# A two-block fp32 network on one core: halved peer_v weights ahead of their tiles, a chunk-major gather, slot gates on expert outputs, and an early memory norm

## The chip, the cores and the metric

One NeuronCore of a Trainium2 chip. The metric is the device time of one execution in microseconds (us); lower is better. Engines are called PE (TensorE), ACT (ScalarE), DVE (VectorE), POOL (GpSimd) and SP (SyncE, which here only issues DMAs).

## What is computed

256 tokens of width 1024 pass through two transformer blocks, all in fp32. The parts that matter here, cut from the reference:

```python
# block 1: stick-breaking attention and spatial gating, then 4 groups x 8 experts (1024 x 512)
combine = (g_onehot[:, :, None] * (g_weight[:, None] * e_w)[:, None, :]).astype(x.dtype)  # top 1 group, top 2 experts
for g in range(N_GROUPS):
    h = silu(einsum('nd,edf->nef', xt, w_gate[g])) * einsum('nd,edf->nef', xt, w_up[g])
    out = out + einsum('nef,efd->nd', h * combine[:, g, :, None], w_down[g])
# block 2
merged = sigmoid(gate_a) * (o_a @ w_branch_a) + sigmoid(gate_b) * (o_b @ w_branch_b)
h = h + merged @ w_out
h = h + memory_cross_attention(rms_norm(h, norm_cross), rms_norm(mem, norm_mem), w_cross_q, w_cross_kv, w_cross_o)
# peer_ffn: 16384 experts; each token takes 16 of them in each of 8 heads
act = gelu(einsum('cd,chkd->chk', xc, u_tab[ec]))
out = einsum('chk,chkd->cd', gc * act, v_tab[ec])
```

## The kernel before, in words

**Products.** A full fp32 product on PE is four passes. Most large products here are three fp32r matmuls instead (`three`, L194): each operand is split into a rounded HIGH part, which ACT copies (`high_quarters` L173, `high` L1713, `weight_high` L1993), and a LOW rest, which DVE subtracts (`low_quarters` L180, `low` L1730, `weight_low` L2032). The experts' own weights stay plain fp32. All matmuls are issued at L189 (`mm`), all transposes at L192 (`tr`).

**Order.** Every engine has its program written out by hand; `Steps` numbers the steps of an engine on one semaphore, and others wait for a step with `.at(name)`. SP loads all large weights in one order through slots of 2 MB (`load_piece` L165).

**Experts (143 to 663 us).** Expert `ex` owns 64 slots. For each, `experts_pe` (L585) runs gate and up (32 fp32 matmuls, 8 chunks x 2 x 2; the trace has two records for each fp32 matmul), `add(ex-1)` (L610: the 64x128 placing matrix times the output rows of the expert before, into four banks that gather all experts), two transposes of h, the turning of the placing matrix `PC` (one-hot x gate weight `CB`, made by `places_dve` L739), a quarter of the gather of the next four experts (`gather_pe` L576: 8 matmuls whose weights are the halved normed tokens, `XGH` and `XH` in the rows, read at every 8th column), and the product with w_down (y). ACT does silu and the copy `hp` (h turned and placing turned); DVE does h = silu x up, the gathered rows, and `YS`, the copy of y. Three weight pieces of 2 MB per expert come through seven slots.

**Seam and mixers of block 2 (663 to 905 us).** After the last add DVE adds four 128x512 residual pieces (L804), the norm follows, and PE starts on block 2's input projection in pieces b0 to b9 of w_in. High and low of b0 and b1 stand at the end of the experts' code.

**Branches and cross attention (905 to 1058 us).** `branches`: for each half of the tokens four products with w_branch, each followed by DVE's `sa`, `sb`, `sx`. Then `cross_pe` (L1428): turn of the merged rows, w_out in two halves (`residual`, o20 and o21), with the turn of the normed memory `turnm` between, K of the memory (kv0), turn of the normed tokens, V (kv1), Q (cq). mem is loaded at L1481 ff. by ACT's queue after the last merged row.

**Dense PEER (1121 to 1950 us).** 128 "up" tiles of peer_u, then 128 "down" tiles of peer_v. SP loads tile i, ACT makes TH (three buffers), DVE makes TL (five buffers). An up tile's gelu goes to DRAM (`g_hold`) and comes back in the down phase into `GL` (four buffers); POOL multiplies it by the router's weights `C`; ACT makes WH and DVE WL (two buffers each), the weights of the down tile's 12 matmuls of 128x512. The loops of ACT and DVE:

```python
for i in range(255):                       # ACT
    if i + 2 < 256:
        high(act, i + 2)                   # TH of tile i+2
    if i >= 127:
        weight_high(i - 127)               # WH of down tile i-127; waits for down tile i-129
for i in range(lows_made.count, 257):      # DVE
    if i < 256:
        low(dve)                           # TL of tile i
    if i >= 129:
        weight_low(i - 129)                # WL of down tile i-129
```

`high(act, i + 2)` waits until the tile three before it has been used, so both steps of ACT in one turn of the loop wait for the same down tile of PE. SP issues the read of g_hold for down tile j when it comes to tile j+129, behind a wait for the WL of four tiles before.

## Time and profile before

| what | us |
|---|---|
| three runs | 1958.85, 1956.11, 1966.63 |
| their median | 1958.85 |
| the profiled execution's own time | 1964.08 |
| its span | 1962.3 |
| PE busy | 1814.5 (92%) |
| DVE, ACT, POOL busy | 927.3, 680.3, 310.2 |
| mean granted TensorE clock, of full speed | 0.954 |

The page cuts the span into 40 slices of 49 us, a digit for the busy tenths:

```profile
PE   6977999999999598999878999999999999999997
...
PEclk9987999999999897579989999999999999999999
DMA  7128999999999435013433177755556766666664
```

PE is busy nearly throughout. DMA is at nine tenths only in slices 5 to 13, the experts; it has room elsewhere. The clock falls below nine tenths between slice 14 and slice 19, in the seam and the mixers of block 2. A matmul's row shows its latency in the pipeline, so the spacing of the starts of a run of matmuls, not a row's mean, tells what each costs.

### The profile page before, as it was taken

Reading aid. Unit: us, or ns where it says so; the run is one execution under the profiler, and the core shown is the slowest. Engines: PE = TensorE matmul, PEld = TensorE weight load, DVE = VectorE, ACT = ScalarE, POOL = GpSimd, SP = SyncE. Lnnn points to the kernel's source line nnn. Section 1 sums busy time; section 2 is a strip of 40 time slices with the busy share of each in tenths; the row PEclk is TensorE's granted clock in tenths of the full one; section 3 lists DMA queues with packets and bytes.
Section 4 is the critical chain, followed back from the end, with each engine's and each line's share of the span. In section 5 each row is a group of like instructions: output and inputs, shape, how many; then the busy total and the mean of one; then the engine's idle time right before and its main releaser. Section 6 shows DMA issues by size and latency. Waiting matters only on the chain.

```text
span 1962.3 us, 27788 instructions
## 1 busy us (share of the span) xinstructions
PE 1814.5 (92%) x11296; PEld 1402.2 (71%) x11296; DVE 927.3 (47%) x1753; ACT 680.3 (35%) x1143; POOL 310.2 (16%) x289
## 2 busy tenths in 40 slices
PE   6977999999999598999878999999999999999997
PEld 6765555555555396566676999999999766666665
DVE  4533111111111433654524899666665566666665
ACT  5720000000000243452334444555554444444443
...
PEclk9987999999999897579989999999999999999999
DMA  7128999999999435013433177755556766666664
GB/s 312 67 98 367 393 403 413 398 403 408 406 402 418 179 129 215 1 44 129 193 129 118 54 229 228 217 176 175 176 176 188 232 208 207 203 206 203 207 203 130
DMA packets 99651, 443.60 MB, mean 226 GB/s; under 512 B 10432, under 2 KB 43712, under 8 KB 79424
## 3 DMA queue, kind: packets, MB, share of 16 engines
...
## 4 chain that ended last, share of the span: by engine, by line
PE 82%; DVE 9%; ACT 6%; DMA 1%; issue 1%; ACTq 0%; DVEq 0%
PE PS L189 79%; DVE TL L1734 4%; PE PS L192 3%; ACT TH L1717 3%; DVE WL L2034 1%; DMA AR<-in_mem 1%; DVE LO L185 1%; ACT HI L178 0%; DMA AR<-in_w_out 0%; DVE XL L248 0%; ACT XSs L255 0%; DMA Hs<-in_x 0%; DVE Wk L261 0%; DVE AR L261 0%; DVE Wk L1352 0%
## 5 line engine op out<-in xcount | busy, mean ns | idle before, releaser
L1734 DVE TENSOR_TENSOR TL<-Wk,TH 128x1024 fp32r<-128x1024 f32 x256 | 357.9, 1398 | 280.1 <-ACT TH L1717 280.0
L1717 ACT ACTIVATE TH<-Wk 128x1024 fp32r<-128x1024 f32 x256 | 270.1, 1055 | 230.6 <-PE PS L189 230.6
L189 PE MATMUL PS<-XH,TH 128*128 128x256 f32 x1024 | 295.1, 288 | 0.8 <-DVE TL L1734 0.8
L189 PE MATMUL PS<-XL,TH 128*128 128x256 f32 x1024 | 289.6, 283 | 0.0
L189 PE MATMUL PS<-XH,TL 128*128 128x256 f32 x1024 | 289.5, 283 | 0.0
L189 PE MATMUL PS<-TH,WH 128*128 128x512 f32 x512 | 211.7, 414 | 25.7 <-DVE WL L2034 22.7
L189 PE MATMUL PS<-AR,Wk 128*64 128x512 f32 (+5 forms) x848 | 216.2, 587 | 6.0 <-ACT Wk L685 2.1
L189 PE MATMUL PS<-AR 128*64 128x256 f32 (+2 forms) x1912 | 208.2, 389 | 6.1 <-ACT AR L1192 2.5
L189 PE MATMUL PS<-TH,WL 128*128 128x512 f32 x512 | 202.7, 396 | 0.0
L189 PE MATMUL PS<-TL,WH 128*128 128x512 f32 x512 | 202.2, 395 | 0.0
L189 PEld LDWEIGHTS PS<-XH,TH 128*128 128x128 f32 x1024 | 196.2, 192 | 1.0 <-DVE TL L1734 1.0
L189 PEld LDWEIGHTS PS<-XL,TH 128*128 128x128 f32 x1024 | 196.4, 192 | 0.0
L189 PEld LDWEIGHTS PS<-XH,TL 128*128 128x128 f32 x1024 | 196.1, 191 | 0.0
L189 PEld LDWEIGHTS PS<-AR 128*64 128x64 f32 (+1 forms) x1912 | 134.5, 141 | 85.1 <-issue 18.4
L2072 POOL TENSOR_TENSOR CO<-CO,AR 128x256 f32<-128x256 f32 x128 | 142.6, 1114 | 304.4 <-DMA CO<-g_hold 304.4
L189 PEld LDWEIGHTS PS<-TH,WH 128*128 128x128 f32 x512 | 96.0, 187 | 91.2 <-DVE TL L1734 44.3
L185 DVE TENSOR_TENSOR LO<-AR,HI 128x1024 fp32r<-128x1024 f32 x96 | 111.6, 1226 | 102.1 <-ACT HI L178 102.1
L189 PEld LDWEIGHTS PS<-AR,Wk 128*64 128x64 f32 (+2 forms) x848 | 79.4, 168 | 108.9 <-issue 95.3
L683 ACT ACTIVATE AR<-PS 128x256 f32<-128x256 f32 x32 | 12.3, 383 | 392.5 <-PE PS L189 392.5
L2018 POOL TENSOR_SCALAR RW<-CO,Wk 128x128 f32<-128x128 f32 x128 | 104.1, 823 | 183.2 <-PE PS L189 129.1
L189 PEld LDWEIGHTS PS<-TH,WL 128*128 128x128 f32 x512 | 96.2, 188 | 23.1
L1987 ACT ACTIVATE Wk<-PS 128x256 f32<-128x256 f32 x128 | 49.1, 384 | 179.9 <-PE PS L189 179.8
...
## 6 DMA issues: line engine op xcount, KB each, us to landing
Wk<-in_peer_u SPq DMA_DIRECT2D x128, 512.0 KB, 3.8
Wk<-in_peer_v SPq DMA_DIRECT2D x128, 512.0 KB, 3.8
...
g_hold<-Wk SPq DMA_DIRECT2D x128, 128.0 KB, 3.7
CO<-g_hold SPq DMA_DIRECT2D x128, 128.0 KB, 3.7
```

The costliest lines, as they stand in the source:

```text
L185: eng.tensor_tensor(lo[:, cs], w[:, cs], hi[:, cs].bitcast(F32), ALU.subtract).then_inc(*steps.up(f"{name}.{k}"))
L189: return pe.matmul(o, l, r, start=start, stop=stop, skip_group_check=True)
L192: return pe.transpose(o, i, ident[0:n, 0:n])
L683: act.activation(SG[:, b, :], G[:, 0:256], ACT.Silu).then_inc(*m_act.up(f"silu{ex}"))
L1717: act.activation(TH[:, i % 3], RAW[:, i % 5], ACT.Copy).then_inc(t_high, 1)
L1734: dve.tensor_tensor(TL[:, i % 5], RAW[:, i % 5], TH[:, i % 3].bitcast(F32), ALU.subtract).then_inc(*lows_made.up())
L1987: act.activation(GE[i % 3], P(4 + i % 4)[:, 0:256], ACT.Gelu).then_inc(gelu_done, 1)
L2018: return eng.tensor_scalar(o, io, I1T[:, tok:tok + 1], GTT[:, tok:tok + 1], ALU.is_equal, ALU.mult)
L2034: dve.tensor_tensor(WL[:, j % 2, :], GL[j % 4], WH[:, j % 2, :].bitcast(F32), ALU.subtract).then_inc(w_low, 1)
L2072: pool.tensor_tensor(GL[j % 4], GL[j % 4], C[:, :, j], ALU.mult).then_inc(gated, 1)
```

## The change

- **Dense down.** ACT makes WH ahead of TH, DVE makes WL ahead of TL. GL has seven buffers in place of four, and SP reads g_hold three tiles earlier.
- **Experts.** The normed tokens are written in chunk-major order (one DVE operation per half reads H at every 8th column), so the gather and the first transposes read contiguous columns. PC is gone; the one-hot matrix PG itself is turned, and DVE copies it rounded into PT2 (`hr`). The gate weight of each slot is summed by four matmuls of one column (`gate_of_slots`), which DVE copies to SLOT_GATE (`gs`) before it makes h; y is multiplied by it and halved: ACT writes YH, DVE YL. `add` is then two fp32r matmuls (YH, YL) for each of its four pieces in place of one fp32 matmul.
- **Seam.** The halving of b0 moves into the last expert, b1's high behind it and b1's low behind the split of the turned tokens (`turn_dve` x).
- **Memory.** mem is loaded by SP right after the first block's norm, normed while PE does the gate pieces b6 to b9, and turned between the two halves of the branches. kv0 takes o20's place in the order of loads; its products come first in cross_pe, V comes before the turn of the normed tokens.

Cut to what matters (list names, waits of the same kind and the layout of buffers are left out):

```diff
-                    t = mm(pe, o[:, k, :], halves[n % 2][:, tt, 2 * s + k::8], PG[:, b, tt, :], n == 0, n == 3)
+                    t = mm(pe, o[:, k, :], halves[n % 2][:, tt, (2 * s + k) * 128:(2 * s + k) * 128 + 128], PG[:, b, tt, :], n == 0, n == 3)
...
-                        t = tr(pe, bank[:, k, tt * 128:(tt + 1) * 128], XS[:, tt, 2 * pair + k::8])
+                        t = tr(pe, bank[:, k, tt * 128:(tt + 1) * 128], XS[:, tt, (2 * pair + k) * 128:(2 * pair + k) * 128 + 128])
...
                         r = slice(64 * j, 64 * j + 64)
-                        t = mm(pe, P(2 * tt + j), HP[r, b, 256 + tt * 128:384 + tt * 128], YS[r, b, :], ex == 0, ex == 31)
+                        to = PT2[r, b, tt * 128:tt * 128 + 128]
+                        mm(pe, P(2 * tt + j), to, YH[r, b, :], ex == 0, False)
+                        t = mm(pe, P(2 * tt + j), to, YL[r, b, :], False, ex == 31)
                 t.then_inc(*m_pe.up(f"add{ex}"))
+            def gate_of_slots(ex):
+
+                g, k4 = ex // 4, ex % 4
+                if ex:
+                    pe.wait_ge(*m_dve.at(f"hr{ex - 1}"))
+                for tt in range(2):
+                    pg = PG[:, g % 2, tt, k4 * 64:k4 * 64 + 64].bitcast(F32)
+                    for j in range(2):
+                        t = mm(pe, P(5 - ex % 2)[64 * j:64 * j + 64, 0:1], pg, CB[:, tt, ex:ex + 1], tt == 0, tt == 1)
+                t.then_inc(*m_pe.up(f"gsum{ex}"))
...
-                if ex >= 2:
-                    pe.wait_ge(*m_act.at(f"hp{ex - 2}"))
...
+                gate_of_slots(ex)
                 pe.wait_ge(*m_dve.at(f"h{ex}"))
...
                 for tt in range(2):
-                    pc = PC[:, g % 2, tt, k4 * 64:k4 * 64 + 64]
+                    pg = PG[:, g % 2, tt, k4 * 64:k4 * 64 + 64].bitcast(F32)
                     for j in range(2):
-                        t = mm(pe, G[64 * j:64 * j + 64, 256 + tt * 128:384 + tt * 128], pc, ident, True, True)
+                        t = mm(pe, G[64 * j:64 * j + 64, 256 + tt * 128:384 + tt * 128], pg, ident, True, True)
                 t.then_inc(*m_pe.up(f"turned{ex}"))
...
+                if ex == 31:
+                    act.wait_ge(*m_pe.at("gate31"))
+                    high_quarters(act, "b0", b_act, range(3))
                 act.wait_ge(*m_pe.at(f"up{ex}"))
                 act.activation(SG[:, b, :], G[:, 0:256], ACT.Silu).then_inc(*m_act.up(f"silu{ex}"))
                 act.wait_ge(*m_pe.at(f"turned{ex}"))
-                act.activation(HP[:, b, :], G, ACT.Copy).then_inc(*m_act.up(f"hp{ex}"))
-            act.wait_ge(*m_pe.at("gate31"))
-            high_quarters(act, "b0", b_act)
-            act.wait_ge(*m_pe.at("up31"))
+                act.activation(HP[:, b, :], G[:, 0:256], ACT.Copy).then_inc(*m_act.up(f"hp{ex}"))
+                if ex == 31:
+                    high_quarters(act, "b0", b_act, range(3, 4))
+                act.wait_ge(*m_pe.at(f"y{ex}"))
+                act.activation(YH[:, b, :], P(6), ACT.Copy, scale=SLOT_GATE[:, b:b + 1]).then_inc(*m_act.up(f"ysh{ex}"))
...
-                dve.wait_ge(*m_dve.at(f"pg{g}.{tt}"))
-                dve.tensor_tensor(pc, pg.bitcast(F32), bc(CB[:, tt, 4 * g:4 * g + 4].unsqueeze(2), [128, 4, 64]), ALU.mult).then_inc(
-                    *m_dve.up(f"pc{g}.{tt}"))
...
-                t = scaled(dve, XS[:, tt, :], H[:, tt, :], ST[:, tt:tt + 1])
+                by_chunk = H[:, tt, :].rearrange("p (n c) -> p c n", c=8)
+                t = scaled(dve, XS[:, tt, :].rearrange("p (c n) -> p c n", c=8), by_chunk, ST[:, tt:tt + 1])
...
+                if ex == 31:
+                    low_quarters(dve, "b0", b_act, b_dve, range(2))
+                dve.wait_ge(*m_pe.at(f"gsum{ex}"))
+                dve.tensor_copy(SLOT_GATE[:, b:b + 1], P(5 - b)[:, 0:1]).then_inc(*m_dve.up(f"gs{ex}"))
                 dve.wait_ge(*m_act.at(f"silu{ex}"))
                 dve.tensor_tensor(HM[:, b, :], SG[:, b, :], P(4 + b)[:, 256:512], ALU.mult).then_inc(*m_dve.up(f"h{ex}"))
+                dve.wait_ge(*m_act.at(f"hp{ex}"))
+                dve.tensor_copy(PT2[:, b, :], P(4 + b)[:, 256:512]).then_inc(*m_dve.up(f"hr{ex}"))
                 if g < 7:
                     gathered_dve(dve, g + 1, k4)
-                dve.wait_ge(*m_pe.at(f"y{ex}"))
-                dve.tensor_copy(YS[:, b, :], P(6)).then_inc(*m_dve.up(f"ys{ex}"))
-            low_quarters(dve, "b0", b_act, b_dve)
-            low_quarters(dve, "b1", b_act, b_dve)
+                if ex == 31:
+                    low_quarters(dve, "b0", b_act, b_dve, range(2, 4))
+                dve.wait_ge(*m_act.at(f"ysh{ex}"))
+                dve.scalar_tensor_tensor(YL[:, b, :], P(6), SLOT_GATE[:, b:b + 1], YH[:, b, :].bitcast(F32), ALU.mult,
+                                         ALU.subtract).then_inc(*m_dve.up(f"ys{ex}"))
...
-            for name, step in (("b2", m_pe.at("up30")), ("b3", m_pe.at("y30")), ("b4", b_pe.at("q3")), ("b5", b_pe.at("k3")),
+            for name, step in (("b2", m_pe.at("up30")), ("b3", m_pe.at("y30"))):
+                sp.wait_ge(*step)
+                load_piece(sp, name)
+            sp.wait_ge(*m_dve.at("normed"))
+            sp.dma_start(MM, mem.rearrange("(t p) d -> p t d", p=128)).then_inc(ld_mem, 16)
+            for name, step in (("b4", b_pe.at("q3")), ("b5", b_pe.at("k3")),
                                ("ck0", b_pe.at("va1")), ("ck1", b_pe.at("qb3")), ("b6", b_pe.at("kv3")), ("b7", b_pe.at("vb1")),
                                ("b8", b_pe.at("cmp")), ("b9", b_pe.at("cmp")), ("wa", b_pe.at("g01")), ("wb", b_pe.at("g11")),
-                               ("o20", b_pe.at("g21")), ("o21", b_pe.at("g31"))):
+                               ("kv0", b_pe.at("g21")), ("o20", b_pe.at("g31"))):
...
+                if tt == 0:
+                    pe.wait_ge(*b_dve.at("mem"))
+                    pe.wait_ge(*b_act.at("g31"))
+                    turn_pe(pe, MM).then_inc(*b_pe.up("turnm"))
...
+            act.wait_ge(ld_mem, 16)
+            square_sum(act, MM[:, 0, :], junk[:, 0, :], ST[:, 24:25]).then_inc(*b_act.up("sqm"))
...
+                if j == 0:
+                    act.wait_ge(*b_dve.at("meanm"))
+                    act.activation(ST[:, 24:26], ST[:, 24:26], ACT.Sqrt).then_inc(*b_act.up("rootm"))
...
+            high_quarters(act, "kv0", b_act)
+            act.wait_ge(*b_pe.at("turnm"))
+            turn_act(act, MX2, sm["g_mem"], b_act, "m")
             high_quarters(act, "o20", b_act)
-            high_quarters(act, "o21", b_act)
...
             turn_dve(dve, X2, sm["g_nmix"], b_act, b_dve, "x")
+            low_quarters(dve, "b1", b_act, b_dve)
             lam = sm["lam"]
             for i in range(2):
                 t = dve.tensor_tensor_reduce(S4[:, i, 0:64], lam[:, 128 * i:128 * i + 64], lam[:, 128 * i + 64:128 * i + 128], 1.0, 0.0,
...
-            for name in ("b7", "b8", "b9", "o20", "o21"):
-                low_quarters(dve, name, b_act, b_dve)
+            dve.wait_ge(ld_mem, 16)
+            square_sum_dve(dve, MM[:, 1, :], junk[:, 1, :], ST[:, 25:26]).then_inc(*b_dve.up("ssm"))
+            dve.wait_ge(*b_act.at("sqm"))
...
+            for tt in range(2):
+                t = scaled(dve, MM[:, tt, :], MM[:, tt, :], ST[:, 24 + tt:25 + tt])
+            t.then_inc(*b_dve.up("mem"))
...
+            branches(0)
+            low_quarters(dve, "kv0", b_act, b_dve)
+            turn_dve(dve, MX2, sm["g_mem"], b_act, b_dve, "m")
+            branches(1)
+            low_quarters(dve, "o20", b_act, b_dve)
...
-            for name, step in (("kv0", b_pe.at("b11")), ("kv1", b_pe.at("b11")), ("cq", c_pe.at("r01")), ("co", c_pe.at("r11")),
-                               ("pq0", c_pe.at("k3")), ("pq1", c_pe.at("v1"))):
+            for name, step in (("o21", b_pe.at("b11")), ("kv1", b_pe.at("b11")), ("cq", c_pe.at("k3")), ("co", c_pe.at("r01")),
+                               ("pq0", c_pe.at("r11")), ("pq1", c_pe.at("v1"))):
                 sp.wait_ge(*step)
...
         def cross_pe(pe):
+            for m in range(4):
+                if m >= 2:
+                    pe.wait_ge(*c_act.at(f"k{m - 2}"))
+                turned(pe, "kv0", MX2, P(m % 2)[:, 0:256], m, *((b_dve, b_dve, "m") if m == 0 else ())).then_inc(*c_pe.up(f"k{m}"))
             pe.wait_ge(*b_dve.at("sx11"))
+            pe.wait_ge(*c_act.at("k3"))
             turn_pe(pe, XS).then_inc(*c_pe.up("turnx"))
-
-            def residual(j):
+            for j, lows in ((0, b_dve), (1, c_dve)):
                 for tt in range(2):
-                    tokens(pe, f"o2{j}", X2, P(4 + 2 * j + tt), tt, *((b_dve,) if tt == 0 else ()),
+                    tokens(pe, f"o2{j}", X2, P(4 + 2 * j + tt), tt, *((lows,) if tt == 0 else ()),
                            *((c_dve, "x") if j + tt == 0 else ())).then_inc(*c_pe.up(f"r{j}{tt}"))
-
-            residual(0)
-            pe.wait_ge(*c_dve.at("mem"))
-            turn_pe(pe, MM).then_inc(*c_pe.up("turnm"))
-            residual(1)
+            for tt in range(2):
+                tokens(pe, "kv1", MX2, P(tt), tt, *((c_dve,) if tt == 0 else ())).then_inc(*c_pe.up(f"v{tt}"))
+            pe.wait_ge(*c_dve.at("zs"))
+            pe.wait_ge(*c_act.at("v1"))
+            turn_pe(pe, XS).then_inc(*c_pe.up("turnz"))
             for m in range(4):
-                pe.wait_ge(*(c_act.at(f"k{m - 2}") if m >= 2 else c_dve.at(f"r0{m}")))
-                turned(pe, "kv0", MX2, P(4 + m % 2)[:, 0:256], m, *((c_dve, c_dve, "m") if m == 0 else ())).then_inc(*c_pe.up(f"k{m}"))
-            pe.wait_ge(*c_dve.at("zs"))
-            turn_pe(pe, XS).then_inc(*c_pe.up("turnz"))
-            for tt in range(2):
-                pe.wait_ge(*c_dve.at(f"r1{tt}"))
-                tokens(pe, "kv1", MX2, P(6 + tt), tt, *((c_dve,) if tt == 0 else ())).then_inc(*c_pe.up(f"v{tt}"))
-            for m in range(4):
-                pe.wait_ge(*c_act.at(f"q{m - 2}" if m >= 2 else f"k{m + 2}"))
+                pe.wait_ge(*(c_act.at(f"q{m - 2}") if m >= 2 else c_dve.at("r11")))
...
-                j = i - 129
+                j = i - 126
                 if 0 <= j < 128:
                     if j == 0:
                         sp.wait_ge(pairs, 64)
                     sp.wait_ge(g_out[j % 3], 16 * (j // 3 + 1))
-                    if j >= 4:
-                        sp.wait_ge(w_low, j - 3)
-                    sp.dma_start(GL[j % 4], g_hold[j]).then_inc(g_in[j % 4], 16)
+                    if j >= 7:
+                        sp.wait_ge(w_low, j - 6)
+                    sp.dma_start(GL[j % 7], g_hold[j]).then_inc(g_in[j % 7], 16)
...
             for i in range(255):
+                if i >= 127:
+                    weight_high(i - 127)
                 if i + 2 < 256:
                     high(act, i + 2)
                 if i == LOWS_BEFORE_SUB:
                     gates_exp_act(act)
-                if i >= 127:
-                    weight_high(i - 127)
...
             for i in range(lows_made.count, 257):
+                if i >= 129:
+                    weight_low(i - 129)
                 if i < 256:
                     low(dve)
                 if 0 <= i - TAKE - 1 < 64:
                     marks(i - TAKE - 1)
-                if i >= 129:
-                    weight_low(i - 129)
```

On ACT, where the up tiles change to the down tiles; TH is the high part of a table tile, WH that of a down tile's weights, and the writes to Wk or RW from PS are gelus. Before:

```order
L1717 ACTIVATE TH<-Wk 128x1024
L1987 ACTIVATE Wk<-PS 128x256
L1717 ACTIVATE TH<-Wk 128x1024
L1997 ACTIVATE WH<-CO 128x256
L1987 ACTIVATE Wk<-PS 128x256
L1717 ACTIVATE TH<-Wk 128x1024
L1997 ACTIVATE WH<-CO 128x256
```

and now:

```order
L2024 ACTIVATE RW<-PS 128x256
L2034 ACTIVATE WH<-CO 128x256
L1754 ACTIVATE TH<-Wk 128x1024
L2024 ACTIVATE RW<-PS 128x256
L2034 ACTIVATE WH<-CO 128x256
L1754 ACTIVATE TH<-Wk 128x1024
L2034 ACTIVATE WH<-CO 128x256
```

The WH copy stands ahead of the TH copy of its turn; behind the last gelu the two alternate in both kernels.

On PE, one expert between gate/up and the gather. Before:

```order
L189 MATMUL PS<-AR,Wk 64x512 x8
L189 MATMUL PS<-AR 64x256 x32
L189 MATMUL PS<-AR,Wk 128x512 x4
L192 MATMUL PS<-CO,AR 128x128 x2
L189 MATMUL PS<-CO,Wk 64x128 x4
L189 MATMUL PS<-PG,XGH 128x256
```

and now:

```order
L189 MATMUL PS<-AR,Wk 64x512 x8
L189 MATMUL PS<-AR 64x256 x32
L189 MATMUL PS<-YH,PT_59 128x512
L189 MATMUL PS<-YL,PT_59 128x512
...
L189 MATMUL PS<-Wk,PG 64x1 x4
L192 MATMUL PS<-CO,AR 128x128 x2
L189 MATMUL PS<-CO,PG 64x128 x4
L189 MATMUL PS<-PG,XGH 128x256
```

YH and YL alternate four times. The four matmuls of one column are new and stand between the add and the transposes of h.

On DVE, the last expert and the seam (AR written from PS is h, L797 the copy of y, Hs the residual, LO the low parts of w_in, XL that of the turned tokens). Now:

```order
L185 TENSOR_TENSOR LO_51<-AR,HI_49 128x1024 x2
L811 COPY Wk<-PS 128x1
L813 TENSOR_TENSOR AR<-AR,PS 128x256
L815 CAST PT_59<-PS 128x256
L185 TENSOR_TENSOR LO_51<-AR,HI_49 128x1024 x2
L821 SCALAR_TENSOR_TENSOR YL<-PS,Wk,YH 128x512
L827 TENSOR_TENSOR Hs<-PS,Hs 128x512 x4
...
L248 SCALAR_TENSOR_TENSOR XL<-PS,SM,XH 128x256 x8
L185 TENSOR_TENSOR LO_52<-AR,HI_50 128x1024 x4
```

Before, all eight lows of L185 stood between the copy of y and the residual adds; now four stand ahead of it and four behind the split of the turned tokens.

## Rows read from the trace of the kernel before

**Rows 1.** Table by stretch: us; busy and count of each engine; clock, DMA share, GB/s

```profile
521.61:537.00 15.39, 15.39 (x107) 9.01 (x106) 1.99 (x4) 0.98 (x2) 0.00 (x0) 1.00 1.00 412
1540.00:1950.00 410.00, 385.13 (x1536) 278.59 (x1536) 257.19 (x254) 171.97 (x253) 140.86 (x126) 1.00 0.65 201
```

**Rows 2.** Groups by line, down phase 1540 to 1950: busy us, mean ns, idle before

```profile
L189 PE MATMUL PS<-TH,WH 128*128 128x512 f32 x512 | 211.7, 414 | 25.7 <-DVE WL L2034 22.7 <-issue 0.9
L1734 DVE TENSOR_TENSOR TL<-Wk,TH 128x1024 fp32r<-128x1024 f32 x126 | 191.4, 1519 | 146.9 <-ACT TH L1717 146.9
L2072 POOL TENSOR_TENSOR CO<-CO,AR 128x256 f32<-128x256 f32 x126 | 140.9, 1118 | 261.5 <-DMA CO<-g_hold 261.5
```

**Rows 3.** Timeline of one down tile: start, duration (us), engine, what, idle before

```profile
1700.44 1.06 ACT L1717 ACTIVATE TH<-Wk 128x1024 fp32r<-128x1024 f32 x1 [2.20 <-PE PS L189]
1700.67 0.40 PE L189 MATMUL PS<-TL,WH 128*128 128x512 f32 x1
1700.80 0.88 POOL L2072 TENSOR_TENSOR CO<-CO,AR 128x256 f32<-128x256 f32 x1 [0.87 <-DMA CO<-g_hold]
1701.41 0.40 ACT L1997 ACTIVATE WH<-CO 128x256 fp32r<-128x256 f32 x1
1701.54 1.23 DVE L1734 TENSOR_TENSOR TL<-Wk,TH 128x1024 fp32r<-128x1024 f32 x1 [1.33 <-ACT TH L1717]
1702.68 0.41 DVE L2034 TENSOR_TENSOR WL<-CO,WH 128x256 fp32r<-128x256 f32 x1
1703.00 0.40 PE L189 MATMUL PS<-TH,WL 128*128 128x512 f32 x1
```

**Rows 4.** Timeline of one expert, PE and the h of DVE

```profile
356.51 7.08 PE L189 MATMUL PS<-AR 128*64 128x256 f32 x64
363.52 1.99 PE L189 MATMUL PS<-AR,Wk 64*128 64x512 f32 x8
364.05 0.42 DVE L793 TENSOR_TENSOR AR<-AR,PS 128x256 f32<-128x256 f32 x1 [5.05 <-ACT AR L683]
365.44 0.50 PE L192 MATMUL PS<-CO,AR 128*128 128x128 f32 x2
366.46 0.51 PE L189 MATMUL PS<-PG,XGH 128*128 128x256 f32 x1
368.60 3.65 PE L189 MATMUL PS<-AR,Wk 128*64 128x512 f32 x16
372.08 3.62 PE L189 MATMUL PS<-Wk,AR 128*64 128x256 f32 x32
```

**Rows 5.** Groups of weight loads on PE, whole kernel: busy us, mean ns, idle before

```profile
L189 PEld LDWEIGHTS PS<-XH,TL 128*128 128x128 f32 x1024 | 196.1, 191 | 0.0
L189 PEld LDWEIGHTS PS<-PG,XH 128*128 128x128 f32 x128 | 43.3, 339 | 0.0
```

**Rows 6.** Timeline of SP and DVE, last experts and seam

```profile
626.90 0.38 SPq L171 DMA_DIRECT2D Wk<-in_w_down  x1
...
662.59 0.69 DVE L797 COPY AR<-PS 128x512 f32<-128x512 f32 x1 [6.46 <-PE PS L189]
663.20 9.16 DVE L185 TENSOR_TENSOR LO<-AR,HI 128x1024 fp32r<-128x1024 f32 x8
672.28 2.47 DVE L804 TENSOR_TENSOR Hs<-PS,Hs 128x512 f32<-128x512 f32 x4
...
688.22 3.23 DVE L248 SCALAR_TENSOR_TENSOR XL<-PS,SM,XH 128x256 fp32r<-128x256 f32 x8 [5.03 <-ACT XH L241]
```

**Rows 7.** Timeline of PE from the branches to the cross attention

```profile
920.67 14.00 PE L189 MATMUL PS<-AR,Wk 128*128 128x512 f32 x32 [1.38 <-DVE AR L1385]
936.18 2.06 PE L192 MATMUL PS<-CO,XSs 128*128 128x128 f32 x16 [1.50 <-DVE XSs L1387]
955.38 3.68 PE L192 MATMUL PS<-CO,AR 128*128 128x128 f32 x16 [4.38 <-DVE AR L261]
```

**Rows 8.** Chain of waits, the one piece between those rows: start, us, what

```profile
936.15 14.83 DMA AR<-in_mem
```

**Rows 9.** Page, DMA issues of this kind: count, KB each, us to landing

```profile
CO<-g_hold SPq DMA_DIRECT2D x128, 128.0 KB, 3.7
```

146 lines of the change are left out of this document (69 added, 77 removed).

## The prediction

> **What bounds the kernel now.** I read the table by stretch first, then the groups by line, the timelines, and the chain of waits last. The span is PE's nearly everywhere, so a part gains only where it takes matmuls off PE or closes a gap on it. Two long stages stand out. In the experts a stretch of 15.39 us has PE busy throughout and the DMAs at their full share, 412 GB/s [rows 1]: PE and DMA both bind. In the down phase PE is busy 385.13 of 410.00 us with DMA at 0.65 [rows 1], and one group carries the idle time, 25.7 us in front of the matmuls by WH, nearly all released by DVE's WL [rows 2]. The busy time hides more than that. From the second matmul of a tile (1700.67) to its twelfth (1703.00) there are ten steps of 0.233 us [rows 3], so a tile needs 12 x 0.233 = 2.80 us, and it gets 410.00/128 = 3.20. The other 0.2 us per tile lie in the last matmul's row, which lasts 0.40 while the next could start after 0.233.
>
> **Dense down.** What makes a tile late: when PE has done tile j-2, ACT may write TH of tile j+1 and only then WH of tile j (1700.44 and 1701.41); on DVE the low of the table (1.23 us, 1.519 on average) stands before WL (1702.68) [rows 2, 3]. In series that is 1.06 + 1.23 + 0.41 and handovers of about 0.15 = 2.85 us at best, 3.14 with the mean of TL, and PE has only tile j-1, 2.80 us, to do meanwhile. Handovers on PE make it 3.20. Afterwards the chain from tile j-2 is WH 0.40 + WL 0.41 + handovers, about 1 us, or 1.9 if POOL's 0.88 [rows 3] stands in its way. Either is under 2.80. TH and TL fall back by 0.4 us, but TH has three buffers and is needed a whole tile later: done(j-2) + 0.40 + 1.06 + 1.52 = 3.0 us, against 5.6 until tile j+1 begins. Nothing on ACT (1.46 us a tile) or DVE (1.93 to 2.11) is near 2.80. So PE becomes the bound; I take 2.82 a tile: 128 x (3.20 - 2.82) = **-48.6 us**. Bounds: -25.7, only the idle time of the group [rows 2], and -51. The longer ring of GL is costed at nothing: POOL waits for its reads (261.5 us [rows 2]), but a read lands in 3.7 us [rows 9] and is issued about two tiles and PE's backlog ahead; it covers the WH copy that is now earlier.
>
> **Experts, per expert.** A period is 372.08 - 356.51 = 15.57 us: gate and up 7.01, add 1.92, transposes and turning 1.02, gather 2.14, y 3.48 [rows 4].
> - add: four fp32 matmuls of four passes take 1.92, so 16 passes at 0.12: the two 64-row halves run beside each other. Now 8 passes of 0.233 in 4 slots plus a tail of 0.18 are 1.11: -0.81. Bound: no overlap, 8 x 0.233, nothing gained.
> - gate_of_slots: four fp32 matmuls of one column. The nearest row is the group of two transposes and four turning matmuls, 1.02 [rows 4]; four sixths are 0.68. With one column in place of 128 I take 0.30; bounds 0.1 and 0.68.
> - h: it used to run under the add (364.05, before 365.44 [rows 4]). It now waits for the sums and for `gs`, so PE's transposes wait: the drain of the last matmul 0.17 to 0.25, gs at most 0.42 (h itself has 256 columns and takes 0.42 [rows 4]) and taken as 0.2, h 0.42: +0.9 of idle PE; bounds 0.7 and 1.2.
> - gather: 8 matmuls of 256 columns. Half of 0.233 would do, but each takes 0.24: the weight load takes 339 ns where contiguous ones take 191 [rows 5]. If the load shrinks, 8 x 0.12 = 0.96 goes; bound: nothing goes.
> - YH, YL, PT2 and HP lie on ACT and DVE under 7 us of gate and up: nothing. SP's queue keeps its order.
>
> Sum -0.81 + 0.30 + 0.90 - 0.96 = -0.57 for each of the 28 experts that gather, -16.0. The last four have no gather: +0.39, less 0.22 since y there waits for the copy hp, now half as wide (a 128x1024 copy takes 1.06 and a 128x256 one 0.40 [rows 3], 0.22 for 256 columns): +0.7. At the start PC goes (-0.4) and the normed tokens are written from a strided read (+0.7). **-15.0 us.** Bounds -27 and +12.
>
> Here a page speaks against part of it. The 16 transposes at 936.18 read at stride 8 too and take 2.06 us, 0.13 each [rows 7]; a load of 339 ns has no room there. So stride alone does not set the price, and whether the gather's loads shrink is open. The Trainium skill (SBUF — State Buffer, section "Door 1", its note on cachelines) says that each access that leaves a 16-byte line pays, so that fp32 can be strided by up to 4 elements for free. By it the gather gains, as I took; the transposes would gain too, which that row denies, and DVE's strided read would cost more than I took.
>
> Does DMA allow 15.0? Three pieces of 2 MiB (6.29 MB) at 412 GB/s need 15.27 us. The shortfall of 0.27 adds up to 7.6 us over 28 experts. But the last w_down is issued at 626.90 and is needed at 662.59 - 3.5 = 659.1 [rows 6], while the three pieces under way then need at most 15.3: the lead is 17 us. It covers that.
>
> **Seam.** Eight lows (9.16 us) stand between the copy of y and the residual adds at 672.28 [rows 6]. Four are now done in the last expert and four later, so the adds start when y31, YH, YL and the last add are done: 662.54 + 0.6 + 0.7 + 1.1 + handovers = 665.6: -6.7. b1's four lows (4 x 1.145 = 4.6) now follow DVE's split at 688.22 [rows 6] and hold up the small lambda work, for which ACT's copies of q wait: +2.0, bounds 0 and 4.6. **-4.7 us.**
>
> **Memory and cross.** Gone from PE's path: the wait for `sb` 1.38 and for the merged rows 1.50, the wait for the normed memory 4.38, and part of turnm's 3.68 us, which is so long since the clock had fallen in the 14.83 us in which the path waited for mem [rows 7, 8]; at full clock 16 transposes take 2.06 [rows 7]. That is 1.38 + 1.50 + 4.38 + 1.6 = 8.9, and some 1.8 for the half-speed matmuls behind that wait and for the wait of k. New are waits for the evacuation of k and v (0.45 + 0.7) and for the second norm, with V alone (6 us) to hide it: 1.9. The norm of mem on ACT and DVE hides under PE's gates; if b7's highs come late by a square and two table loads, that costs 1 to 2 us, which I put into the range. **-8 us**, bounds -2 and -12.
>
> **Sum**: 48.6 + 15.0 + 4.7 + 8 = 76.3, so 1964.1 - 76.3 = 1887.8 against the profiled execution's own time. The median of the runs shown stands 5.2 below that time, which would give 1882.6. I forecast **1885**.
>
> **Rivals.**
> - *The experts gain nothing.* Either the gather keeps its 0.24 a matmul (28 x 0.96 = 27 us back), for which the transposes speak, or the halves of the add do not overlap in their new order YH, YL of one half, then of the other (31 x 0.81 = 25 back), against which only the 1.92 of the fp32 order speaks. 1910.
> - *The down phase gives only its idle time.* The tails of 0.2 a tile stay, because each tile ends with a handover: 48.6 - 25.7 = 23 back, 1908. For it: the busy time of PE, if read plainly. Against: within a tile the same matmuls follow each other after 0.233.
> - *Slower.* WH(j), which waits for POOL's product and so for the read of g_hold, now stands ahead of TH(j+1) on ACT. If a read comes late, the table is held up too. A read issued only when it is needed costs 3.7 + 1.1 + 0.40 + 1.06 + 1.52 = 7.8 us for two tiles, 3.9 a tile: 128 x (3.9 - 3.2) = +90, with the other parts 1964 + 90 - 28 = 2026. It decides if a read needs more than its lead, some five tiles or 14 us; the 3.7 to landing [rows 9] speaks against it.
> - *More than forecast.* All parts near their better bounds (down -51, experts -22, cross -11): 1870.
>
> **How the numbers follow.** Main case 0.62, experts without gain 0.16, down with its idle time alone 0.11, more 0.07, slower 0.04. The main case's own spread is 1872 to 1900, from the idle time of PE in an expert (28 x 0.25) and the bounds of seam and cross. The range **1860 to 1918** takes in the two single disappointments and the better case, and leaves out both disappointments together and the slower case. About 10 us (0.5%) is what a measurement of this kernel can tell from no change: 1949 and 1969 are the borders. Faster 0.94; same 0.03 (both disappointments and a worse cross); slower 0.03.
>
> **What would show it.** Down: no idle time released by WL, the stretch 1540 to its end about 361 us long for the 128 tiles, PE's idle in it under 3. Experts: starts of gate 15.0 apart; rows of the gather's matmuls 0.12 apart with loads of about 190 ns; add 1.1 long; a gap of 0.9 before the transposes of h, released by DVE's h. Seam: residual adds 3 us behind y31; a gap by the lambda work. Cross: no wait for mem, turnm between the branches at 2 us. If the down phase stays over 3.0 a tile with ACT released by POOL, the slower case's mechanism is at work; if experts start 15.5 or more apart, the step that failed is the gather or the add, and the spacing of their rows says which.

## The result and the profile after

The changed kernel takes 1874.07 us (median of four runs, 1867.24 to 1876.08), the kernel before, measured in the same sessions, 1962.74. The ratio is 0.9536, 95% interval 0.9506 to 0.9566: 4.6% or some 90 us faster. The profiled execution took 1873.55 us against 1964.08, its span is 1871.7 against 1962.3. The result lies inside the forecast range of 1860 to 1918, 11 us below the 1885 that was named; in the profiled executions the sum of the forecast gains (76.3 us) was 14 us short of the 90.6 measured.

Executions of one kernel can lie some 10 us apart, as the clock granted in the mixers of block 2 stays low for longer in some (the end of the first Q to the first gate piece took 107.5 us in the profiled execution here and 99.6 in that of the version with the late halving alone, by the same code), so a median of four or five runs can move by several us with no cause in the kernel.

The head of the page and the slices, after:

```profile
span 1871.7 us, 28357 instructions
...
PE 1742.0 (93%) x11552; PEld 1390.9 (74%) x11552; DVE 895.1 (48%) x1801; ACT 696.9 (37%) x1176; POOL 317.1 (17%) x289
...
PEclk9987999999999898579997999999999999999999
DMA  7219999999999635004433077765565787777774
```

PE's own busy time fell by 72.5 us. The granted clock is as before (0.952, before 0.954), so the gain is not the clock's.

Where the gain came from, with both spans cut at the same events (starts of pieces in the two chains of waits; y31 is the last expert's product with w_down, Q, K and V the projections of an attention):

| stretch | before | after | difference | forecast |
|---|---|---|---|---|
| start to the first gather | 159.47 | 159.58 | +0.1 | +0.3 together |
| first gather, first gate and up, to the first transposes of h | 19.17 | 15.30 | -3.9 | with the line above |
| 32 experts, to the end of y31 | 483.95 | 461.45 | -22.5 | -15.3 |
| y31 to the residual adds | 9.69 | 2.77 | -6.9 | -6.7 |
| adds to the end of the first Q | 80.54 | 82.25 | +1.7 | +2.0 |
| to the first gate piece | 108.97 | 107.50 | -1.5 | 0 |
| gates, branches, cross to the end of its Q | 145.88 | 138.39 | -7.5 | -8 |
| to the first down tile | 532.2 | 533.6 | +1.4 | 0 |
| down phase | 410.05 | 358.60 | -51.5 | -48.6 |
| end | 12.35 | 12.3 | 0 | 0 |
| sum | 1962.3 | 1871.7 | -90.6 | -76.3 |

**Down phase.** The table by stretch for one expert and for all down tiles, with the columns of [rows 1]:

```profile
352.15:366.92 14.77, 14.18 (x114) 8.38 (x114) 2.54 (x6) 1.46 (x3) 0.00 (x0) 1.00 1.01 424
1500.80:1859.40 358.60, 358.56 (x1538) 288.40 (x1536) 214.06 (x254) 173.25 (x254) 143.09 (x124) 1.00 0.75 230
```

358.60/128 = 2.80 us a tile, and PE is busy all of it: that is 12 matmuls at the 0.233 us from start to start of the prediction. The groups of this phase, to be read against [rows 2]:

```profile
L189 PE MATMUL PS<-TH,WH 128*128 128x512 f32 x512 | 202.5, 396 | 0.0
L1771 DVE TENSOR_TENSOR TL<-Wk,TH 128x1024 fp32r<-128x1024 f32 x127 | 158.9, 1251 | 64.1 <-ACT TH L1754 64.1
L2109 POOL TENSOR_TENSOR CO<-CO,AR 128x256 f32<-128x256 f32 x125 | 144.9, 1159 | 205.5 <-DMA CO<-g_hold 205.5
L1754 ACT ACTIVATE TH<-Wk 128x1024 fp32r<-128x1024 f32 x127 | 132.7, 1045 | 0.0
L2034 ACT ACTIVATE WH<-CO 128x256 fp32r<-128x256 f32 x128 | 53.9, 421 | 180.0 <-PE PS L189 180.0
```

The 25.7 us in front of the matmuls by WH are 0.0. ACT now waits only in front of WH, and only for PE: its 180.0 us of idle time cost nothing. TL takes 1.251 us on average, 1.519 before. The timeline of one tile, against [rows 3]:

```profile
1699.86 0.42 ACT L2034 ACTIVATE WH<-CO 128x256 fp32r<-128x256 f32 x1 [1.43 <-PE PS L189]
...
1700.18 1.04 ACT L1754 ACTIVATE TH<-Wk 128x1024 fp32r<-128x1024 f32 x1
...
1700.31 0.42 DVE L2071 TENSOR_TENSOR WL<-CO,WH 128x256 fp32r<-128x256 f32 x1 [0.63 <-ACT WH L2034]
...
1701.26 1.23 DVE L1771 TENSOR_TENSOR TL<-Wk,TH 128x1024 fp32r<-128x1024 f32 x1 [0.52 <-ACT TH L1754]
```

From the start of WH, which PE releases, to the end of WL it is 1700.73 - 1699.86 = 0.9 us, as forecast (1 us); from the start of TH to the end of WL it was 1703.09 - 1700.44 = 2.65 [rows 3].

**Experts.** The period, from one expert's transposes of h to the next's, fell from 15.57 to 14.77 us. The timeline of one, against [rows 4]:

```profile
352.15 0.50 PE L192 MATMUL PS<-CO,AR 128*128 128x128 f32 x2 [0.59 <-DVE AR L813]
...
353.17 0.39 PE L189 MATMUL PS<-PG,XGH 128*128 128x256 f32 x1
...
354.31 3.65 PE L189 MATMUL PS<-AR,Wk 128*64 128x512 f32 x16
...
364.81 0.50 PE L189 MATMUL PS<-YH,PT 64*128 64x512 f32 x2
...
365.93 0.40 PE L189 MATMUL PS<-Wk,PG 128*64 128x1 f32 x8
...
366.38 0.16 DVE L811 COPY Wk<-PS 128x1 f32<-128x1 f32 x1 [6.89 <-PE PS L189]
366.46 0.41 DVE L813 TENSOR_TENSOR AR<-AR,PS 128x256 f32<-128x256 f32 x1
```

Add 365.93 - 364.81 = 1.12 (forecast 1.11); sums 0.40 and PE's idle 0.59, together 0.99 (forecast 0.30 + 0.90); gather 354.31 - 353.17 = 1.14 (forecast 1.18). The loads of the gather, against the second line of [rows 5]:

```profile
L189 PEld LDWEIGHTS PS<-PG,XH 128*128 128x128 f32 x104 | 19.5, 188 | 0.0
```

**Seam and cross.** Pieces of the chain of waits (start, us, what), against [rows 6 to 8]:

```profile
636.33 0.70 ACT YH L706
637.05 0.76 DVE YL L821
637.85 1.23 PE PS L189 x8
639.10 0.57 DVE Hs L827
...
655.09 3.23 DVE XL L248 x8
658.32 4.54 DVE LO L185 x4
662.85 0.30 DVE Wk L1310 x4
...
886.39 1.77 PE PS L192 x16
888.16 25.25 PE PS L189 x128
...
913.96 2.03 PE PS L192 x16
```

No lows stand between y31 and the adds; b1's four are now on the path ahead of the lambda work (L1310). The memory is turned at 886.39 in 1.77 us instead of 3.68, no piece waits for mem, and PE runs through to the turn of the merged rows.

### The profile page after: what moved, and what is told of

It is laid out like the page before. It is cut to its first block, busy times and chain, and to the rows that moved or that the text cites. A ratio compares the mean times of both kernels' runs of the same rounds, so it can differ in the third digit from the quotient of the medians.

```text
span 1871.7 us, 28357 instructions
## 1 busy us (share of the span) xinstructions
PE 1742.0 (93%) x11552; PEld 1390.9 (74%) x11552; DVE 895.1 (48%) x1801; ACT 696.9 (37%) x1176; POOL 317.1 (17%) x289
## 3 DMA queue, kind: packets, MB, share of 16 engines
q10 hardware_dynamic: 432, 1.18, 0.2%
## 4 chain that ended last, share of the span: by engine, by line
PE 90%; DVE 5%; ACT 3%; DMA 1%; issue 1%; SPq 0%; ACTq 0%; DVEq 0%
PE PS L189 87%; PE PS L192 3%; DMA AR<-in_w_in 1%; DVE AR L813 1%; ACT HI L178 0%; DVE XL L248 0%; DVE LO L185 0%; DVE Wk L811 0%; DVE Wk L261 0%; ACT XSs L255 0%; DVE Wk L1400 0%; ACT XH L241 0%; ACT AR L1561 0%; DVE NTs L261 0%; DVE Wk L1403 0%
## 5 line engine op out<-in xcount | busy, mean ns | idle before, releaser
L1771 DVE TENSOR_TENSOR TL<-Wk,TH 128x1024 fp32r<-128x1024 f32 x256 | 324.2, 1267 | 195.5 <-ACT TH L1754 195.4
L189 PE MATMUL PS<-TH,WH 128*128 128x512 f32 x512 | 202.5, 396 | 0.0
L2109 POOL TENSOR_TENSOR CO<-CO,AR 128x256 f32<-128x256 f32 x128 | 149.6, 1169 | 239.6 <-DMA CO<-g_hold 239.6
L189 PE MATMUL PS<-AR,Wk 128*64 128x512 f32 (+4 forms) x592 | 152.8, 575 | 3.2 <-ACT Wk L702 1.4
L185 DVE TENSOR_TENSOR LO<-AR,HI 128x1024 fp32r<-128x1024 f32 x96 | 111.7, 1226 | 74.4 <-ACT HI L178 74.4
L2034 ACT ACTIVATE WH<-CO 128x256 fp32r<-128x256 f32 x128 | 53.9, 421 | 180.0 <-PE PS L189 180.0
L189 PE MATMUL PS<-XH,HI 128*128 128x256 f32 x352 | 103.7, 295 | 12.8 <-DVE XL L248 5.8
L189 PEld LDWEIGHTS PS<-AR,Wk 128*64 128x64 f32 (+2 forms) x592 | 57.6, 161 | 77.7 <-issue 68.0
L189 PEld LDWEIGHTS PS<-TL,WH 128*128 128x128 f32 x512 | 96.2, 188 | 23.3
## 6 DMA issues: line engine op xcount, KB each, us to landing
AR<-in_w_down SPq DMA_DIRECT2D x27, 2048.0 KB, 14.7
```

The lines of the kernel that those rows point to most:

```text
L185: eng.tensor_tensor(lo[:, cs], w[:, cs], hi[:, cs].bitcast(F32), ALU.subtract).then_inc(*steps.up(f"{name}.{k}"))
L189: return pe.matmul(o, l, r, start=start, stop=stop, skip_group_check=True)
L1771: dve.tensor_tensor(TL[:, i % 5], RAW[:, i % 5], TH[:, i % 3].bitcast(F32), ALU.subtract).then_inc(*lows_made.up())
L2034: act.activation(WH[:, j % 2, :], GL[j % 7], ACT.Copy).then_inc(w_high, 1)
L2109: pool.tensor_tensor(GL[j % 7], GL[j % 7], C[:, :, j], ALU.mult).then_inc(gated, 1)
```

## The experiments

Sessions differ a little, so all ratios are to the kernel before, measured in the same session.

### The order of the dense loops alone

```diff
             for i in range(255):
+                if i >= 127:
+                    weight_high(i - 127)
                 if i + 2 < 256:
                     high(act, i + 2)
...
-                if i >= 127:
-                    weight_high(i - 127)
...
             for i in range(lows_made.count, 257):
+                if i >= 129:
+                    weight_low(i - 129)
                 if i < 256:
                     low(dve)
...
-                if i >= 129:
-                    weight_low(i - 129)
```

> Kernel before with nothing but the order of ACT's and DVE's loops in the dense part changed: WH ahead of TH, WL ahead of TL; four GL buffers and the late read of g_hold stay. Theory A (the order is the whole cause): the down phase falls from 410 us to about 359 (12 matmuls x 0.233 x 128), the kernel by 51 us, ratio 0.974. Theory B (the reads need the longer ring once WH stands ahead of TH): WH waits for POOL and holds up TH; the gain is less than 30 us, or there is a loss of up to 90, and ACT's TH shows idle time released by POOL.

0.9747 (0.9706 to 0.9788), 1912.93 us. The stretch of the down phase:

```profile
1534.00:1893.70 359.70, 358.09 (x1525) 285.03 (x1523) 229.42 (x252) 170.93 (x251) 157.22 (x126) 1.00 0.74 228
```

Theory A holds: 359.7 us with four buffers and the late read. But theory B's mechanism is there in small. The chain of waits runs through a read of g_hold and POOL's product at five places, of which this is one:

```profile
1594.00 4.99 DMA CO<-g_hold
1599.06 1.94 POOL CO L2072
```

In this stretch ACT's WH waited 134.1 us for POOL's product, but PE only 1.6 us in all.

### The ring and the earlier read alone

```diff
-        GE = [wk(256) for _ in range(3)]
-        GL = [CO[:, 128 + 256 * k:384 + 256 * k] for k in range(4)]
+        GE = [RW[:, 1536:1792], RW[:, 1792:2048], wk(256)]
+        GL = [CO[:, 128 + 256 * k:384 + 256 * k] for k in range(7)]
...
-                j = i - 129
+                j = i - 126
...
-                    if j >= 4:
-                        sp.wait_ge(w_low, j - 3)
+                    if j >= 7:
+                        sp.wait_ge(w_low, j - 6)
```

> Kernel before with nothing but the seven GL buffers, the read of g_hold three tiles earlier and the buffers' new places; both orders stay. Theory A: no change, within 0.5%, the down phase stays at 410 us, since the late wait is WL behind TL. Theory B (POOL's product came late before): POOL has its data earlier, and the down phase gains 10 to 50 us.

0.9997 (0.9978 to 1.0017), 1964.2 us. The group that carries the wait, and POOL's:

```profile
L189 PE MATMUL PS<-TH,WH 128*128 128x512 f32 x512 | 211.8, 414 | 24.6 <-DVE WL L2034 22.3 <-issue 0.8
...
L2072 POOL TENSOR_TENSOR CO<-CO,AR 128x256 f32<-128x256 f32 x124 | 143.5, 1157 | 250.9 <-DMA CO<-g_hold 250.9
```

The wait is as in [rows 2]; POOL's 250.9 us of waiting for g_hold held up nobody. Theory A holds.

### The whole dense part

Both diffs above.

> Kernel before with the whole dense part of the change (orders and ring), nothing else. Theory A: as with the order alone, -51 us, ratio 0.974. If the ring adds something, this one is faster than the order alone by more than 5 us.

0.972 (0.9691 to 0.9749), 1910.27 us, 2.7 us from the order alone and well within its interval. In the trace the down phase takes 358.60 us where the order alone took 359.70, and WH no longer waits for POOL: the ring is worth about 1 us, too little to see in the run times.

### The experts' part alone

The lines of the change from `gather_pe` to `YL`, without those on b0, on the kernel before; the core of them:

```diff
-                        t = mm(pe, P(2 * tt + j), HP[r, b, 256 + tt * 128:384 + tt * 128], YS[r, b, :], ex == 0, ex == 31)
+                        to = PT2[r, b, tt * 128:tt * 128 + 128]
+                        mm(pe, P(2 * tt + j), to, YH[r, b, :], ex == 0, False)
+                        t = mm(pe, P(2 * tt + j), to, YL[r, b, :], False, ex == 31)
...
                     add(ex - 1)
+                gate_of_slots(ex)
                 pe.wait_ge(*m_dve.at(f"h{ex}"))
```

> Kernel before with the experts' part alone: chunk-major tokens, slot gates, YH and YL; the halving of b0 and b1 stays where it was, memory and dense part too. Theory A (the part is worth what the two traces show side by side): experts 22.5 us shorter, their start 4.6 us shorter, the seam about +0.8 (YH and YL behind y31 in place of one copy): -26 us, ratio 0.987. Theory B (the early halving of b0 or the other parts helped the experts): under 20 us.

0.9914 (0.9887 to 0.9941), 1946.57 us: -17 us, between the two theories, with the interval from -11 to -22. In the trace the experts are 461 us long, as in the changed kernel, so nothing of the other parts is needed for them. The rest of the 26 us is partly missing, and the trace says where: the first gather starts 2.7 us later (162.15 against 159.47), of which 1.9 us are there at 21.18 us, ahead of any edited line; the adds come 1.1 us later behind y31; and the stages from there to the dense part took some 4 us more than before, by code that was not edited. The first and the last are differences between executions, as far as the traces show: in the profiled executions of all versions the first gather starts between 159.0 and 163.2 us.

### The seam alone

```diff
+                if ex == 31:
+                    act.wait_ge(*m_pe.at("gate31"))
+                    high_quarters(act, "b0", b_act, range(3))
                 act.wait_ge(*m_pe.at(f"up{ex}"))
...
-            low_quarters(dve, "b0", b_act, b_dve)
-            low_quarters(dve, "b1", b_act, b_dve)
             dve.wait_ge(*m_pe.at("add31"))
...
             turn_dve(dve, X2, sm["g_nmix"], b_act, b_dve, "x")
+            low_quarters(dve, "b1", b_act, b_dve)
```

> Kernel before with the moved halving of b0 and b1 alone. Theory A (what the two traces show side by side): the residual adds start 7 us sooner behind y31, and b1's four lows in front of the lambda work give 1.7 us back on the way to the end of the first projection: -5 us, ratio 0.9973, stretch from the first turn of block 2 to its first attention 1 to 2 us longer. Theory B (the wait for b1's lows only moves to PE further on): under 2 us, ratio above 0.999.

0.9978 (0.9966 to 0.999), 1957.32 us: -4.3 us. From y31 to the end of the first Q it is 748.63 - 663.63 = 85.0 us, before 90.2. Theory A holds.

### Memory and cross alone

The lines of the change from `mixers2_sp` to `cross_pe`, without b1's, on the kernel before; the core of them:

```diff
+            sp.wait_ge(*m_dve.at("normed"))
+            sp.dma_start(MM, mem.rearrange("(t p) d -> p t d", p=128)).then_inc(ld_mem, 16)
...
+                if tt == 0:
+                    pe.wait_ge(*b_dve.at("mem"))
+                    pe.wait_ge(*b_act.at("g31"))
+                    turn_pe(pe, MM).then_inc(*b_pe.up("turnm"))
```

> Kernel before with the early memory norm and the new order of the cross attention alone. Theory A: from the first gate piece to the end of Q 138.4 us in place of 145.9, so -7.5 us, ratio 0.996. Theory B (the early work also changes what stands before the gates, where the change was 1.5 us faster): -9 us. Theory C (the gain came from a higher clock, which the other parts brought): under 3 us.

0.9965 (0.9943 to 0.9988), 1958.2 us: -6.9 us by the ratio, with an interval from -2 to -11; the medians alone differ by 3.8. The run times would leave all three theories open. The trace decides: from the first gate piece to the end of Q it is 1002.91 - 864.58 = 138.3 us, as in the changed kernel and 7.6 less than before. Theory A holds for the stretch, without any of the other parts. The ratios of the four parts (dense, experts, seam, memory) multiplied give 0.958, with intervals that reach the 0.9536 of the whole.

### The strided gather in the changed kernel

```diff
-                    t = mm(pe, o[:, k, :], halves[n % 2][:, tt, (2 * s + k) * 128:(2 * s + k) * 128 + 128], PG[:, b, tt, :], n == 0, n == 3)
+                    t = mm(pe, o[:, k, :], halves[n % 2][:, tt, 2 * s + k::8], PG[:, b, tt, :], n == 0, n == 3)
...
-                by_chunk = H[:, tt, :].rearrange("p (n c) -> p c n", c=8)
-                t = scaled(dve, XS[:, tt, :].rearrange("p (c n) -> p c n", c=8), by_chunk, ST[:, tt:tt + 1])
+                t = scaled(dve, XS[:, tt, :], H[:, tt, :], ST[:, tt:tt + 1])
```

> The changed kernel with the normed tokens again in token-major order: the gather's and the first transposes' weights are read at every 8th column, the write of the tokens is contiguous. Theory A (the stride of the weights sets the load's time in the gather): loads of the gather back at 339 ns, its matmuls 0.24 apart, 0.96 us more in each of 28 experts and 2.4 in the first gather, -0.8 for the write: +28 us against the changed kernel, ratio to before 0.968. Theory B (the stride is not the cause, since the transposes at the same stride do not pay): no difference, 0.954.

0.9884 (0.9859 to 0.9908), 1936.96 us: not 28 but some 68 us slower than the changed kernel by the ratios (0.0348 x 1962), and 58.8 us between the two profiled executions, of which 55.3 lie in the experts and 2.4 in the first gather. The loads are back, so the stride is their cause:

```profile
L189 PEld LDWEIGHTS PS<-PG,XH 128*128 128x128 f32 x96 | 32.5, 339 | 0.0
```

That explains the first part, 28 x 0.99 us. In the chain the first seven periods are 15.76 us each, +0.99 on 14.77, as expected; the next 21, from 288 us on, are 17.07; the last four experts, which have no gather, take 14.18 as in the changed kernel. The table by stretch shows why, first inside one of these experts, then the whole of it:

```profile
390.18:392.00 1.82, 1.82 (x13) 1.53 (x14) 0.27 (x1) 0.38 (x1) 0.00 (x0) 1.00 1.01 432
392.00:394.00 2.00, 2.00 (x8) 1.51 (x9) 0.61 (x3) 0.00 (x0) 0.00 (x0) 0.62 0.92 389
394.00:396.00 2.00, 2.00 (x8) 0.49 (x6) 0.42 (x2) 0.00 (x0) 0.00 (x0) 0.52 1.03 426
396.00:398.00 2.00, 2.00 (x12) 0.69 (x10) 0.00 (x0) 0.00 (x0) 0.00 (x0) 1.00 0.82 344
...
390.18:407.25 17.07, 16.48 (x114) 9.56 (x114) 2.54 (x6) 1.46 (x3) 0.00 (x0) 0.90 0.90 368
```

In each of these 21 experts the granted clock falls to its lower level, 1.2 GHz, during the gather and is back at 2.4 GHz some 4 us later; y takes 4.86 us instead of 3.65. The kernel before has the same gather and keeps its clock; the changed kernel has the same gap of 0.59 us and keeps it too.

### h ahead of the slot gates

```diff
-                dve.wait_ge(*m_pe.at(f"gsum{ex}"))
-                dve.tensor_copy(SLOT_GATE[:, b:b + 1], P(5 - b)[:, 0:1]).then_inc(*m_dve.up(f"gs{ex}"))
                 dve.wait_ge(*m_act.at(f"silu{ex}"))
                 dve.tensor_tensor(HM[:, b, :], SG[:, b, :], P(4 + b)[:, 256:512], ALU.mult).then_inc(*m_dve.up(f"h{ex}"))
+                dve.wait_ge(*m_pe.at(f"gsum{ex}"))
+                dve.tensor_copy(SLOT_GATE[:, b:b + 1], P(5 - b)[:, 0:1]).then_inc(*m_dve.up(f"gs{ex}"))
```

> The changed kernel with DVE's h ahead of the copy of the slot gates, so that PE's transposes no longer wait for the sums; ACT and PE wait for the copy where they need it. PE's idle 0.59 us per expert goes. Theory A (PE alone bounds the experts): 32 x 0.59 = 18.9 us faster than the changed kernel, ratio to before 0.944. Theory B (DMA has become the second bound: it already runs at 424 GB/s, and the last w_down lands about 12 us before its use): only about 12 us, ratio 0.9475; the last experts then wait for their weights, the first ones have a period of 14.18, the mean is near 14.4 to 14.8.

0.9564 (0.954 to 0.9587), 1875.77 us: nothing gained, which neither theory expected. The chain of waits shows both why theory B was near and what it missed:

```profile
503.69 8.53 PE PS L189 x61
512.22 14.69 DMA AR<-in_w_up
526.97 14.71 DMA AR<-in_w_up
...
616.15 10.20 DMA AR<-in_w_in
```

For 23 experts the period is 14.11. Then each waits for its w_up, and the period is that of three transfers, 14.7 us: the lead is used up, DMA binds. What DMA still left as a gain was lost at 616.15: b0 comes behind the experts' weights, its high stands on ACT ahead of the last silu and two of its lows on DVE ahead of the last h, and PE waited 9.0 us for that h.

### h first, and b0 and b1 halved late

On top of the edit above: no halving in the last expert; ACT makes b0's high after the last YH; DVE makes b0's low while PE turns the normed tokens; ACT makes three quarters of b1's high there; the lambda work stands ahead of b1's low.

```diff
-            high_quarters(act, "b1", b_act)
+            high_quarters(act, "b0", b_act)
...
             act.activation(XS[:, 0, :], H[:, 0, :], ACT.Copy, scale=ST[:, 0:1]).then_inc(*b_act.up("xs0"))
+            high_quarters(act, "b1", b_act, range(3))
...
+            low_quarters(dve, "b0", b_act, b_dve)
             turn_dve(dve, X2, sm["g_nmix"], b_act, b_dve, "x")
-            low_quarters(dve, "b1", b_act, b_dve)
```

> The changed kernel with h ahead of the copy of the slot gates, and the halving of b0 and b1 taken out of the experts: b0's high behind YH of the last expert, its low while PE turns the normed tokens, b1's high there too, the lambda work ahead of b1's low. Theory A (with h first, DMA bounds the experts at 14.74 us each, and what gave the gain back was ACT's and DVE's wait for b0, 10.2 us, ahead of silu and h of the last expert): the last expert ends some 10 to 13 us sooner than in the changed kernel, the halving is hidden under the norm and the turn, and the kernel is 10 to 13 us faster, ratio to before about 0.948. Theory B (the end of the transfers sets the seam in any case, since b0 is needed for the first product): 0 to 3 us, 0.9525.

0.9497 (0.9466 to 0.9527), 1863.66 us, the fastest of all. The chain at the seam:

```profile
600.65 14.69 DMA AR<-in_w_up
615.38 5.13 PE PS L189 x48
...
622.02 3.68 PE PS L189 x16
625.78 0.70 ACT YH L703
626.50 0.76 DVE YL L814
627.31 1.21 PE PS L189 x8
628.54 0.56 DVE Hs L820
```

From the first gather to the end of y31 it is 625.78 - 162.47 = 463.3 us, in the changed kernel 636.33 - 159.58 = 476.8: 13.4 us less, and no wait for b0. By the ratios 7.7 us arrive, and the intervals of this version and of the changed kernel overlap.

The same kernel in another session, since the intervals overlap:

> The version with h first and the late halving once more, unchanged, in a session of its own, since its interval (0.9466 to 0.9527) still overlaps that of the changed kernel (0.9506 to 0.9566). Theory A (the last expert ends 13 us sooner and nothing gives it back): ratio 0.9485 again, within 0.002. Theory B (the first session was a lucky one and the gain is under 3 us): 0.952 or more.

0.9499 (0.9462 to 0.9536), 1861.64 us. Again 7.3 us by the ratios, a little short of what theory A said; the interval alone would not rule theory B out. The two traces do: from the first gather to the end of y31 it is 463.3 and 463.1 us against 476.8, and the whole executions span 1860.9 and 1858.7 us against 1871.7, so 10.8 and 13.0 us less. In the first session 2.9 us were lost ahead of the first gather (162.47 against 159.58), where the code is the same.

### The late halving without h first

The late halving of the version above on the changed kernel; h stays behind the copy of the gates.

> The changed kernel with the halving moved as above, h still behind the slot gates. Theory A: the adds keep their place (about 3 us behind y31), the lambda work no longer holds up ACT: 0 to 3 us faster than the changed kernel, ratio 0.9525. If this is as fast as the version with h first, h first is worth nothing and DMA sets the end. If it is slower than the changed kernel, DVE's four lows of b0 do not fit beside the turn of the tokens (3.7 us).

0.9534 (0.9504 to 0.9565), 1867.71 us: no difference from the changed kernel, and the same 476.7 us from the first gather to the end of y31. Theory A holds. The late halving pays together with h first; without it nothing can be measured.

### The strided gather with h first

The two edits together.

> The changed kernel with both the strided gather and h first. With the strided gather alone the period was 15.76 us in the first eight experts and 17.07 in the others, where the granted clock fell to its lower level in each gather. Theory A (PE's gap of 0.59 us ahead of the strided gather is what lets the clock fall; the kernel before has the strided gather without the gap and keeps its clock): the clock stays, period 15.1 throughout, 1887 us, ratio 0.962. Theory B (the clock falls by the strided gather together with the shorter add, whatever the gap): still near 16.5 in most experts, above 1915 us, ratio over 0.976.

0.9613 (0.9584 to 0.9642), 1883.98 us, 3 us from what theory A said: the period is 15.10 in all 28 experts with a gather, and the clock stays.

```profile
390.00:406.00 16.00, 16.00 (x124) 9.84 (x122) 3.05 (x7) 1.69 (x4) 0.00 (x0) 1.00 1.00 414
```

Theory A holds. Closing a gap of 0.59 us an expert was worth 53 us here (1936.96 against 1883.98), of which 48 lie in the experts: some 20 are the gap itself (15.76 to 15.10 in 31 periods), 27.5 the clock (21 x 1.31). The rest is no effect of the edit that can be shown: from the end of y31 to the first gate piece the two profiled executions took 193.7 and 184.6 us, by the same code.

## Why the prediction was right, and where its terms were off

- **Down, -48.6 forecast, -51.5 measured.** The reason was right in each part: the order alone brings it (0.9747), the ring alone nothing (0.9997) and beside the order about 1 us, and a tile takes the 12 x 0.233 us of its matmuls. I had left 0.02 us a tile for handovers; there are none. The rival that only the 25.7 us of idle time would go is out: the tails of 0.2 us in the matmul rows went too. (The 2.11 us a tile that the prediction gives DVE as an upper figure come from no row; its busy time was 257.19/128 = 2.01 [rows 1].)
- **The slower case** did not come. With four buffers and the late read, so with less lead than the change gives, its mechanism showed (WH waited for POOL's product, at five places behind a read of g_hold), but it cost PE 1.6 us and not 90. The ring, costed at nothing, takes that away.
- **Experts, -15.3 forecast, -22.5 measured.** The mis-sized term is the wait for the slot gates, taken as the drain of the last matmul, gs at 0.2 and h at 0.42 one after the other, +0.9. gs took 0.16, h began 0.08 after gs had begun, and sums and wait together were 0.99 instead of 0.30 + 0.90 = 1.20: 28 x 0.21 = 5.9 of the 7.2 us. Add (1.12, forecast 1.11) and gather (1.14, forecast 1.18) were right, so both halves of the rival in which the experts gain nothing are out. With the measured sizes the terms make -0.80 + 0.99 - 1.00 = -0.81 an expert; the period fell by 0.80.
- **The gather's stride.** I took the load's 339 ns as the stride's doing against the transposes, which do not pay. The run with the stride put back shows it: 188 against 339 ns. The note on cachelines in the Trainium skill (SBUF — State Buffer, section "Door 1"), by which each access to a new 16-byte line pays, agrees with these loads. It does not agree with the transposes: the first turn of the normed tokens reads at stride 8 in the kernel before and contiguously in the changed one, and its loads took 221 and 222 ns. Why the two kinds of load differ was not tried.
- **DMA, "it covers that".** It did, but the premise was wrong: 412 GB/s was not the transfers' limit. Over the experts they ran at 405 GB/s before, 417 with the strided gather and h first, and 424 in the changed kernel, and 6.29 MB over the periods of 15.57, 15.10 and 14.77 us are 404, 417 and 426: in these three the rate followed the period, at a busy share of about 1.00 in each. Only with h first did PE wait for weights, at 14.7 us an expert; that is the floor, not the 15.27 I had worked out. At 412 GB/s the measured period would have used up 28 x 0.50 = 14 of the 17 us of lead, so that this step held was in part luck.
- **Start, +0.3 forecast, -3.8 measured.** I priced PC and the strided write (2.21 against 1.43 us, +0.8, taken as +0.7) and left the first gather out: its 32 matmuls went from 8.0 to 5.6 us, and the first gate and up from 8.67 to 7.15 us, at a granted clock of 1.00 against 0.82. The 2.4 us are the stride's: with it put back they are lost (8.01). The 1.5 us are less sure: all six profiled executions with the contiguous gather have 7.15, seven with the strided one 8.57 to 10.15, but the eighth, the run with the stride put back alone, has 7.15 too.
- **Seam, -4.7 forecast, -5.2 measured**, by both halves (-6.9, +1.7). Shown alone: -4.3 by the ratio.
- **Memory and cross, -8 forecast, -7.5 measured**, and the same stretch 7.6 shorter with this part alone. PE's waits in the stretch fell from 11.2 to 6.4 us (4.8, forecast 7.3 gone and 1.9 new), turnm from 3.68 to 1.77 (1.9, forecast 1.6); 0.8 is left for the half-speed matmuls, forecast 1.8 with the wait of k. The square and table loads ahead of the gates cost nothing that can be seen.
